# A two-layer attention trunk in one kernel: weight words of the latent section streamed together and added on VectorE, latent keys made two heads at a time

## The reference

```python
h = x @ w_in                                    # (tokens, 1024) @ (1024, ...)
q_lat, ckv, krope, g_mla, dq, dk, dv, g_diff = _split_cols(h, EVEN_SECTIONS)   # 256, 128, 32, 512, ...
q = (_rmsnorm(q_lat, q_g) @ w_uq).reshape(b, s, MLA_HEADS, MLA_QK_DIM)
q_rope = _rope(q[..., MLA_NOPE_DIM:], pos, MLA_ROPE_DIM, MLA_ROPE_THETA)
q_abs = jnp.einsum('bshn,chn->bshc', q[..., :MLA_NOPE_DIM], w_uk)
ckv = _rmsnorm(ckv, kv_g)
krope = _rope(krope, pos, MLA_ROPE_DIM, MLA_ROPE_THETA)
# scores: q_abs . ckv + q_rope . krope, chunk-causal mask, softmax, times ckv, then w_uv
```

## Time and profile before

| | us |
|---|---|
| median of 3 runs | 844.55 (844.47 to 845.53) |
| the profiled execution | 844.67 |
| its span, first to last instruction | 842.9 |
| TensorE matmuls busy | 813.1 (96%) |
| TensorE weight loads busy | 707.9 (84%) |
| VectorE busy | 524.9 (62%) |
| ScalarE busy | 412.1 (49%) |
| GpSimd busy | 74.8 (9%) |

### The profile page before, as it was taken

One profiled execution on the slowest core, in us unless ns is written; L12 is line 12 of the kernel. 1 busy time (PEld: TensorE's weight loads), 2 busy tenths in 40 slices (PEclk: granted clock), 3 DMA queues, 4 the chain that ended last, 5 costly groups with the idle time before them and its releaser, 6 DMA issues.

```text
span 842.9 us, 17104 instructions
## 1 busy us (share of the span) xinstructions
PE 813.1 (96%) x6676; PEld 707.9 (84%) x6676; DVE 524.9 (62%) x1045; ACT 412.1 (49%) x945; POOL 74.8 (9%) x102
## 2 busy tenths in 40 slices
PE   6999999999999999999999999999999999999995
PEld 6996688888888899778899998888988888887674
DVE  4265355665665657766942565666577676778877
ACT  4233533334444456532324555675566665687710
POOL 2120000100000000000310010001100110121002
PEclk9999999999999999999999999999999999999998
DMA  7631211211323334514133334333332333334103
GB/s 234 153 97 50 75 44 52 64 49 42 121 77 105 112 97 134 158 61 137 57 124 109 114 101 140 92 106 110 128 101 91 127 126 115 117 125 132 60 30 125
DMA packets 67533, 86.25 MB, mean 102 GB/s; under 512 B 6016, under 2 KB 53920, under 8 KB 67456
## 3 DMA queue, kind: packets, MB, share of 16 engines
q1 hardware_dynamic: 63712, 74.47, 28.7%
q0 software_dynamic: 3744, 10.70, 4.0%
HBM read 74.25 MB, written 10.90 MB: 101 GB/s over the span
## 4 chain that ended last, share of the span: by engine, by line
PE 80%; issue 9%; DVE 5%; ACT 4%; POOL 2%; DMA 1%; SPq 0%; DVEq 0%; POOLq 0%; ACTq 0%
PE turn L955 24%; PE pair L955 17%; PE value L955 16%; PE proj L955 15%; PE turn L995 3%; PE turn L1171 2%; POOL rstd L928 1%; PE value L995 1%; PE proj L995 1%; PE proj L1171 1%; DVE w_lo L1604 1%; ACT w_hi L1371 1%; DMA x_sb<-in_x_prompt_dram 1%; PE pair L995 1%; DVE probs L1719 0%
## 5 line engine op out<-in xcount | busy, mean ns | idle before, releaser
L1604 DVE TENSOR_TENSOR w_lo<-stage,w_hi 128x512 fp32r<-128x512 f32 (+1 forms) x136 | 91.9, 682 | 114.4 <-ACT w_hi L1371 114.0
L955 PE MATMUL turn<-w_hi,xT_hi 128*128 128x256 f32 (+2 forms) x340 | 106.0, 312 | 1.0 <-DVE xT_lo L1609 0.7
L955 PE MATMUL turn<-w_hi,xT_lo 128*128 128x256 f32 (+2 forms) x340 | 102.5, 301 | 0.0
L955 PE MATMUL turn<-w_lo,xT_hi 128*128 128x256 f32 (+2 forms) x340 | 102.4, 301 | 0.0
L1371 ACT CAST w_hi<-stage 128x512 fp32r<-128x512 f32 (+1 forms) x144 | 87.4, 616 | 19.2 <-PE value L955 6.5
L955 PEld LDWEIGHTS turn<-w_hi,xT_hi 128*128 128x128 f32 x340 | 64.8, 191 | 3.7 <-DVE x_sb L1851 1.5
L955 PEld LDWEIGHTS turn<-w_hi,xT_lo 128*128 128x128 f32 x340 | 64.8, 191 | 2.5
L955 PEld LDWEIGHTS turn<-w_lo,xT_hi 128*128 128x128 f32 x340 | 64.9, 191 | 2.1
L1451 ACT ACTIVATE work<-pair,peak 128x512 f32<-128x512 f32 (+4 forms) x80 | 40.9, 516 | 46.2 <-DVE peak L1708 46.1
L1719 DVE TENSOR_TENSOR_SCAN probs<-probs 128x512 f32<-128x512 f32 (+4 forms) x80 | 61.4, 801 | 1.6
L955 PE MATMUL value<-w_hi,xT_hi 128*128 128x256 f32 (+2 forms) x194 | 60.1, 310 | 0.7 <-DVE w_lo L1604 0.7
(11 more groups left out here) (535 smaller groups left out, 2079.6 us busy)
## 6 DMA issues: line engine op xcount, KB each, us to landing
stage<-in_w_in_odd_dram SPq DMA_DIRECT2D x64, 256.0 KB, 2.7
stage<-in_w_in_even_dram SPq DMA_DIRECT2D x44, 256.0 KB, 2.8
k_c<-in_cache_sb_k_dram SPq DMA_DIRECT2D x32, 256.0 KB, 3.5
v_c<-in_cache_sb_v_dram SPq DMA_DIRECT2D x32, 256.0 KB, 2.9
mlaK<-in_cache_diff_k_dram SPq DMA_DIRECT2D x8, 512.0 KB, 4.1
mlaK<-in_cache_diff_v_dram SPq DMA_DIRECT2D x8, 512.0 KB, 4.5
stage<-in_w_out_even_dram SPq DMA_DIRECT2D x16, 256.0 KB, 2.6
stage<-in_w_out_odd_dram SPq DMA_DIRECT2D x16, 256.0 KB, 2.6
```

The costliest lines, as they stand in the source:

```text
L955: return nc.tensor.matmul(o, l, r, start=first, stop=last)
L1604: v.tensor_tensor(piece(w_lo[:, sec % 2, words]), piece(stage[:, n % STAGES, :]), piece(w_hi[:, sec % 2, words].bitcast(F32)), ALU.subtrac ...
```

## The change

Two edits.

**Two sums.** `w_hi` and `w_lo` become the two halves of one buffer `w_words`. For `A` jobs `project` calls `two_sums`: the high word of the activation is multiplied by high and low weight words in one matmul, whose moving operand is two runs of n columns and whose result is two sums side by side in the bank (2n columns: 512 or 320); the low word of the activation is multiplied by the high weights and added to the left sum. Two matmuls with 3n columns in all stand where three stood. The two sums are added on the way out of the bank: `sum_of` is a reduction over pairs on VectorE, which writes `lat`. ScalarE's copy of `A` jobs is gone.

**Keys of two heads.** `("kn", pair)` is one matmul with the 128 columns of two heads, one job in each of the first four tiles, and fills all 128 partitions of its bank. VectorE still makes two copies of 64 x 512, the second from partitions 64 to 127. The score waits for the pair's job.

```diff
--- before.py
+++ after.py
@@ -169,6 +169,7 @@
 for _g in range(GROUPS):
     SECTIONS += [f"{_kind}{_g}" for _kind in ("kvgq" if _g + 1 < GROUPS else "kvqg")]
 SECTIONS += ["out100", "out110", "out101", "out111"]
+TWO_SUMS = ("A",)
 POOL_SPLITS = range(QUARTERS * (len(SECTIONS) - 4), QUARTERS * (len(SECTIONS) - 2))
 
 
@@ -216,7 +217,7 @@
     for t in tiles:
         jobs += [("uq", t, 0), ("uq", t, 1), ("uqrope", t)]
         if t < PT_TILES:
-            jobs += [("kn", 2 * t), ("kn", 2 * t + 1)]
+            jobs += [("kn", t)]
         jobs += values[t]
         if t:
             jobs += [("qT", t - 1, 0), ("qT", t - 1, 1)]
@@ -437,8 +438,8 @@
 
         xT_hi = sb("xT_hi", [KD, TOK], F32R)
         xT_lo = sb("xT_lo", [KD, TOK], F32R)
-        w_hi = sb("w_hi", [2, KD * HALF], F32R)
-        w_lo = sb("w_lo", [2, KD * HALF], F32R)
+        w_words = sb("w_words", [2, 2, KD * HALF], F32R)
+        w_hi, w_lo = w_words[:, 0], w_words[:, 1]
         stage = sb("stage", [STAGES, 512])
         probs = sb("probs", [3, 512])
         work8 = sb("work8", [4, 512])
@@ -961,6 +962,13 @@
                 mm(o, s_hi, m_lo, False, False)
                 return mm(o, s_lo, m_hi, False, last)
 
+            def two_sums(o, sta, sec, c0, n, first, last):
+
+                s_hi, s_lo = sta
+                words = w_words[:, :, SECTIONS.index(sec) % 2, c0:c0 + n]
+                mm(o[:, 0:2 * n].rearrange("p (a n) -> p a n", a=2), s_hi, words, first, False)
+                return mm(o[:, 0:n], s_lo, words[:, 0], False, last)
+
             def x_block(k, cols):
                 return xT_hi[:, k, cols], xT_lo[:, k, cols]
 
@@ -977,14 +985,16 @@
             def project(job, t):
 
                 wait_bank(pe, job)
-                for i, sec in enumerate(sections_of(job)):
+                for sec in sections_of(job):
                     n = SEC_A - HALF if sec == "A1" else HALF
                     for k in range(KD):
                         wait_quarter(job, sec, k // 2)
                         if job[0] == "A" and k == KD // 2:
                             wait_drained(pe, ("xT", 0, t, 1))
-                        m = product(ps(job)[:, i * HALF:i * HALF + n], x_block(k, tok(t)), w_block(sec, k * HALF, n),
-                                    k == 0, k == KD - 1)
+                        if job[0] in TWO_SUMS:
+                            m = two_sums(ps(job), x_block(k, tok(t)), sec, k * HALF, n, k == 0, k == KD - 1)
+                        else:
+                            m = product(ps(job)[:, 0:n], x_block(k, tok(t)), w_block(sec, k * HALF, n), k == 0, k == KD - 1)
                 m.then_inc(filled[where[job][0]], 1)
 
             def transposes(job, pieces):
@@ -1030,11 +1040,11 @@
                     pe.wait_ge(uq_done, t + 1)
                     transposes(job, [(i * P, uq[:, t % 2, (4 * h + i) * QK:(4 * h + i + 1) * QK]) for i in range(4)])
                 elif kind == "kn":
-                    h = job[1]
+                    pair = job[1]
                     for t in range(PT_TILES):
                         wait_drained(pe, ("latT", t))
                     wait_bank(pe, job)
-                    mm(ps(job)[0:NOPE, :], w_uk[:, h * NOPE:(h + 1) * NOPE], latT[:, 2, 0:SEQ], True, True).then_inc(done, 1)
+                    mm(ps(job)[:, :], w_uk[:, 2 * pair * NOPE:2 * (pair + 1) * NOPE], latT[:, 2, 0:SEQ], True, True).then_inc(done, 1)
                 elif kind == "vm":
                     wait_bank(pe, job)
                     mm(ps(job)[:, :], latT[:, 2, tok(job[1])], w_uv[:, :], True, True).then_inc(done, 1)
@@ -1083,8 +1093,8 @@
                         pe.wait_ge(kr_done, PT_TILES)
                         for j in range(4):
                             wait_drained(pe, ("latT", j))
+                        wait_drained(pe, ("kn", pair))
                         for i in range(2):
-                            wait_drained(pe, ("kn", 2 * pair + i))
                             wait_drained(pe, ("qT", t, i))
                         for i in range(2):
                             h = 2 * pair + i
@@ -1373,10 +1383,6 @@
                     src, ks, cols = heads_of(job)
                     wait_heads(act, job)
                     nc.scalar.copy(xT_hi[:, ks, cols], src[:, ks, cols]).then_inc(ocvt_hi, 1)
-                elif kind == "A":
-                    wait_filled(act, job)
-                    cols = slice(0, HALF) if job[2] == 0 else slice(HALF, SEC_A)
-                    nc.scalar.copy(lat[:, job[1], cols], ps(job)[:, 0:cols.stop - cols.start]).then_inc(done, 1)
                 elif kind in ("G", "gd"):
                     n = silu_no[job]
                     if n > 2:
@@ -1576,6 +1582,11 @@
                 steps_done[0] += 1
                 ins.then_inc(dve_step, 1)
                 dve.wait_ge(dve_step, steps_done[0])
+
+            def sum_of(job, o, n):
+
+                wait_filled(dve, job)
+                return v.tensor_reduce(o, ps(job)[:, 0:2 * n].rearrange("p (a n) -> p n a", a=2), AX_X, ALU.add)
 
             def rotate(x, table, tmp):
 
@@ -1669,11 +1680,15 @@
                     rotate(q_, ropem[:, t:t + 1, :, :, :], tmp).then_inc(uq_done, 1)
                 elif kind == "kn":
                     wait_filled(dve, job)
-                    v.tensor_copy(mlaK[0:NOPE, job[1], :], ps(job)[0:NOPE, :]).then_inc(done, 1)
+                    v.tensor_copy(mlaK[0:NOPE, 2 * job[1], :], ps(job)[0:NOPE, :])
+                    v.tensor_copy(mlaK[0:NOPE, 2 * job[1] + 1, :], ps(job)[NOPE:P, :]).then_inc(done, 1)
                 elif kind == "wukT":
                     wait_filled(dve, job)
                     v.tensor_copy(wukT[0:NOPE, 4 * job[1]:4 * job[1] + 4, :],
                                   ps(job)[0:NOPE, :].rearrange("p (k n) -> p k n", k=4)).then_inc(done, 1)
+                elif kind == "A":
+                    cols = slice(0, HALF) if job[2] == 0 else slice(HALF, SEC_A)
+                    sum_of(job, lat[:, job[1], cols], cols.stop - cols.start).then_inc(done, 1)
                 elif kind in ("dq", "dk"):
                     t, n = job[1], rot_no[job] - 1
                     wait_drained(dve, job)
```

## The result

| | us |
|---|---|
| before, median of 4 runs | 844.51 (844.47 to 845.53) |
| after, median of 4 runs | 834.88 (834.30 to 835.63) |
| ratio, 95% interval | 0.9884 (0.9866 to 0.9901) |
| profiled executions | 844.67 and 834.43, spans 842.9 and 832.6 |

The change gains 9.6 us by the medians and 10.2 us between the profiled executions. The forecast was 837.0, with 835.4 as the lower end of its range: the sign was right, and the gain is about 2 us larger than forecast and lies outside the range.

The account below looks back on a forecast made before the run. TensorE's order of matmuls was taken as the program's clock. Terms of 0.4 + 3.0 + 3.4 + 0.7 = 7.5 us, all before the first score, gave a median of 837.0 us, range 835.4 to 839.6.

Parts of the forecast that it names:

- left half: Latent section, 512 + 256 columns in place of 3 x 256: one start saved per block, 0.4 us over four warm tiles.
- right half: Latent section, 320 + 160 columns in place of 3 x 160: 0.258 us a block in place of 0.333, 3.0 us.
- latent keys: Key products of two heads issued at once: four products fewer at 0.86 us each, 3.4 us.
- ring of banks: PSUM banks ahead of the first score: the shifted order removes TensorE's wait for ScalarE's copy, 0.7 us, at worst zero.
- start of the normalisation: Behind the last latent tile: the normalisation of the latents starts no later against TensorE; no gain counted.
- start of the program: First tile: lower clock level, pitch the columns alone, no gain taken; the added sum free, 0.35 us late at double price.
- after the first score: From the first score to the end: the same stretch as before, 738 us, begun 7.5 us earlier.
- the width of the stationary side costs nothing, the columns streamed do: Latent keys: a product of 64 stationary columns priced like a value product of 128, 0.86 us each.
- rivals 1 and 3: Right half: 1, both weight loads hide, 835.8, chance 0.08; 3, the 0.111 us belong to each 160-column run, 839.5, chance 0.05.
- the fourth rival: Joined matmuls: the two-run moving operand streams in two passes or at half rate, 13.8 us lost, 850.8, chance 0.03.
- Rival 2: Latent keys' stretch paced by other engines' copies and rotations: 3.4 us become TensorE idle time, 840.4, chance 0.06.
- the sums: VectorE: ten sums in place of ten ScalarE copies, 0.69 us left and 0.5 right, hidden so that nobody waits.

Follow-up runs that it names:

- third experiment: Kernel before, still eight latent key products, each with its pair's 128 stationary columns and one half copied out: 843.29 us, ratio 0.9986.
- fourth experiment: Changed kernel, each key job taking two turns of the ring of PSUM banks, so later jobs lie in their former banks: 835.62 us, ratio 0.9898.
- first experiment: Kernel before with the latent section's two sums alone, keys left as eight products of 64 stationary columns: 840.30 us, ratio 0.9950.
- fifth and ninth kernel: Kernel before with extra matmuls on zeroed memory at the start: seven in the fifth, 845.05 us; six smaller in the ninth, 843.75 us.
- the two pairs: Kernel before and changed kernel, both with extra start matmuls: seven, 845.05 and 835.60 us; six smaller, 843.75 and 834.39 us.
- tenth kernel: Changed kernel with six small extra matmuls on zeroed memory in TensorE's idle time at the start: 834.39 us, ratio 0.9891.

## Why the prediction was wrong

By its own terms, against the 10.3 us by which the profiled span is shorter:

| term | forecast | measured | from |
|---|---|---|---|
| left half | 0.4 | 0.34 | 13.33 - 12.99 |
| right half | 3.0 | 3.02 | 13.37 - 10.35 |
| latent keys | 3.4 | 4.71 | 38.10 - 33.39 |
| ring of banks | 0.7 | 0.86 | 4.30 - 3.44 |
| start of the normalisation | 0 | 0.29 | 5.34 - 5.05 |
| start of the program | 0 | 0.88 | 15.78 - 14.90 |
| after the first score | 0 | 0.2 | (842.9 - 104.66) - (832.6 - 94.56) |

**The step that failed** is "the width of the stationary side costs nothing, the columns streamed do". It priced a key product by the value products, which have 128 stationary columns among neighbours of 128, and took the 1.86 us of a pair, "the switch to the next kind included", for two times 0.86 and some rounding. The switch is a cost of its own: the first weights of 64 columns aren't loaded ahead, and neither are the first 128 behind them. It is 0.34 us a tile in the timelines, and the third experiment gets 1.2 us from it without removing a product. That is 1.2 of the 1.3 us that the term lacks. The rest of the term, 4 x 0.86, was right (3.52 measured).

This step alone does not leave the range: 837.0 - 1.3 is 835.7. With the normalisation (0.29) and the ring (0.16 more than forecast) the five stages ahead of the first score make 9.2 us, and 844.55 - 9.2 = 835.3, at the edge of 835.4. The median of 834.88 lies another 0.4 us lower, of which 0.2 may be the stretch behind the first score and the rest the start; neither is clear of the spread between executions.

**What was right.** The right half, to 0.02 us, and with it the argument that the weight load and not the run of columns sets the 0.111 us: rivals 1 and 3 fall (a block would take 0.227 or 0.320 us; it takes 0.26). By the isolated gap of the Trainium skill, page "TensorE: Matmul & The Clock Gate", section "Back-to-back issue gap", both halves together would have given 0.2 us; the trace shows 3.4. The moving operand in two runs costs nothing visible, so the fourth rival falls. Rival 2 falls with the 33.39 us, of which TensorE is busy for 33.32 (before, 38.02 of 38.10). The ring was right too, confirmed by the fourth experiment, and so were the sums, at 0.69 and 0.49 us, and their cover.

**Smaller misses.** The normalisation was said to start "no later"; it starts 0.43 us sooner behind `dv0`'s first product, since ScalarE's high word no longer stands behind its own copy, and 0.29 us of it reach the queries (the first experiment shows it without the keys; the same stage is 5.47 and 5.49 us in the fifth and ninth kernel, so some 0.15 of it can come and go). The working had that number in hand, 1.46 against 1.1 us, and left it out of the sum. The start of the program differs between profiled executions, by 2 us at the second tile (14.40 to 16.44 among the kernels without added matmuls, the first tile made in the same way in these two), and the level that TensorE's first products run at is part of it. Its part in the medians stays open; by the two pairs it is small.

**The range.** It had no room below for a switch cost, since the term of the keys had its bound on one side only. The trace held the number: the loads' row of the kernel before, with its brackets of 0.55 and 0.81 us, isn't among the rows that the prediction rests on.

## What to carry to other kernels

Read TensorE's weight loads beside its matmuls: a load that starts together with its matmul, where others start one matmul ahead, is a seam. Products with 64 stationary columns among products with 128 had one on either side here, about 0.3 us together, even where nothing else differed; transposes with 96 and 64 had none. So look for the seam in the loads and don't infer it from the width. With 128 stationary rows and columns, a load of 0.11 us was hidden by the matmul before it only where that one streamed longer, so join the narrow ones (160 columns gained 0.07 us a block here, 256 only 0.01). An extra reduction on VectorE was free where TensorE's next need lay behind another transfer or conversion, in the latent section; at the `v` jobs half the gain went into waits.

## What the runs showed of the hardware that was not expected

Narrowing the stationary operand of the key products from 128 to 64 columns, among neighbours of 128, makes TensorE slower, not cheaper (844.50 against 843.29 with 128, third experiment), while transposes with 64 columns run on at 0.11 us each. A visible weight load isn't charged to the matmul whose load it is by the starts of the matmuls: 320 and 160 columns stood 0.19 and 0.07 us apart, where 0.147 and 0.111 were expected, with the same sum. The change from 0.213 to 0.12 us per 256 columns in the first tile came between 10.7 and 13.4 us in the two profiled executions, and is invisible in the granted clock, which reads 1.00 there. The later fall in the tenth kernel, behind 1.79 us without work, is visible in it, at 0.50: a reading of 1.00 at the start of a profile doesn't tell the level, the distance between matmuls does.
